# Norm sums with tokens on partitions: root and reciprocal on a few columns, spread back by products with the identity

## The reference

```python
def rmsnorm(x, g):
    x32 = x.astype(jnp.float32)
    y = x32 * lax.rsqrt(jnp.mean(x32 * x32, axis=-1, keepdims=True) + EPS)
    return (y * g.astype(jnp.float32)).astype(x.dtype)

def layer_norm(x, g, b):
    xf = x.astype(jnp.float32)
    mu = jnp.mean(xf, -1, keepdims=True)
    var = jnp.mean(jnp.square(xf - mu), -1, keepdims=True)
    y = (xf - mu) * lax.rsqrt(var + LN_EPS) * g.astype(jnp.float32) + b.astype(jnp.float32)
    return y.astype(x.dtype)
```

## Time and profile before

| | us |
|---|---|
| median of 3 runs | 2226.37 |
| lowest and highest of them | 2225.61, 2236.63 |
| profiled execution, its own time | 2233.53 |
| profiled execution, span from first to last instruction | 2231.7 |

### The profile page before, as it was taken

The page is one execution under the profiler, slowest core; times in us unless marked ns, Lnnn a source line. Parts: engine busy times, 40 slices in busy tenths (PEclk is TensorE's granted clock), DMA queues, the critical chain, the costliest instruction groups (busy, mean ns, idle before and its releaser), DMA issues. The chain is left out here.

```text
span 2231.7 us, 36800 instructions
## 1 busy us (share of the span) xinstructions
PE 2108.8 (94%) x14195; PEld 1892.5 (85%) x14195; DVE 1483.2 (66%) x2248; ACT 1157.1 (52%) x1655; POOL 26.1 (1%) x34
## 2 busy tenths in 40 slices
PE   7999999999999999889999988999999989999997
PEld 6999897999999978779998977787778758778876
DVE  5665675665666644476564456789888466888896
ACT  4343533534444335464433336678776455777774
POOL 1000000000000020000000000000000000000000
PEclk9999999999999999999999979999999999999999
DMA  8555222654445523334454521599996514799991
GB/s 278 191 196 177 95 82 90 216 179 169 170 170 175 197 80 128 138 114 170 169 186 143 148 73 58 180 328 334 342 317 212 217 38 170 244 318 325 318 358 56
DMA packets 312310, 421.09 MB, mean 189 GB/s; under 512 B 7844, under 2 KB 266304, under 8 KB 312096
## 3 DMA queue, kind: packets, MB, share of 16 engines
q1 hardware_dynamic: 308864, 415.93, 54.5%
q10 hardware_dynamic: 2816, 2.38, 0.5%
q0 software_dynamic: 544, 1.62, 0.2%
HBM read 416.70 MB, written 1.05 MB: 187 GB/s over the span
## 5 line engine op out<-in xcount | busy, mean ns | idle before, releaser
L2816 DVE TENSOR_TENSOR w_lo<-weight_ring,w_hi 128x1024 fp32r<-128x1024 f32 x384 | 449.3, 1220 | 35.9 <-ACT w_hi L2665 31.2
L569 PE MATMUL banks<-x_hi,w_hi 128*128 128x256 f32 x1408 | 401.0, 285 | 8.5 <-DVE w_lo L522 7.7
L570 PE MATMUL banks<-x_lo,w_hi 128*128 128x256 f32 x1408 | 399.3, 284 | 0.0
L571 PE MATMUL banks<-x_hi,w_lo 128*128 128x256 f32 x1408 | 399.3, 284 | 0.0
L2665 ACT ACTIVATE w_hi<-weight_ring 128x1024 fp32r<-128x1024 f32 x384 | 382.3, 1053 | 21.4 <-PE banks L2552 21.3
L515 ACT ACTIVATE w_hi<-weight_ring 128x1024 fp32r<-128x1024 f32 x88 | 93.0, 1057 | 418.5 <-PE banks L571 418.3
L887 DVE TENSOR_TENSOR pieces<-weight_ring,pieces 128x512 fp32r<-128x512 f32 (+2 forms) x245 | 166.3, 689 | 193.8 <-ACT pieces L876 192.3
L876 ACT ACTIVATE pieces<-weight_ring 128x512 fp32r<-128x512 f32 (+2 forms) x245 | 150.9, 627 | 251.3 <-PE banks L823 244.5
L569 PEld LDWEIGHTS banks<-x_hi,w_hi 128*128 128x128 f32 x1408 | 271.2, 193 | 10.8 <-DVE w_lo L522 8.6
L570 PEld LDWEIGHTS banks<-x_lo,w_hi 128*128 128x128 f32 x1408 | 271.3, 193 | 0.1
L571 PEld LDWEIGHTS banks<-x_hi,w_lo 128*128 128x128 f32 x1408 | 271.2, 193 | 0.0
(11 more groups left out here) (367 smaller groups left out, 3907.3 us busy)
## 6 DMA issues: line engine op xcount, KB each, us to landing
weight_ring<-in_ffn_w_in SPq DMA_DIRECT2D x88, 1024.0 KB, 7.5
weight_ring<-in_moe_w_gate SPq DMA_DIRECT2D x64, 1024.0 KB, 6.6
weight_ring<-in_moe_w_up SPq DMA_DIRECT2D x64, 1024.0 KB, 9.2
weight_ring<-in_moe_w_down SPq DMA_DIRECT2D x64, 1024.0 KB, 11.1
weight_ring<-in_ffn_w_out SPq DMA_DIRECT2D x44, 1024.0 KB, 9.6
weight_ring<-in_hg_w_in SPq DMA_DIRECT2D x12, 1024.0 KB, 8.2
weight_ring<-in_fox_w_in SPq DMA_DIRECT2D x12, 1024.0 KB, 8.5
weight_ring<-in_nsa_w_in SPq DMA_DIRECT2D x10, 1024.0 KB, 7.8
```

Of the source, the lines that this page charges most:

```text
L569: pe.matmul(out, w_hi, m_hi, start=start, stop=False, skip_group_check=True)
L570: pe.matmul(out, w_hi, m_lo, start=False, stop=False, skip_group_check=True)
L571: return pe.matmul(out, w_lo, m_hi, start=False, stop=stop, skip_group_check=True)
L2816: dve.tensor_tensor(self.piece(s, p, self.w_lo), self.piece(s, p), self.piece(s, p, self.w_hi.bitcast(F32)), ALU.subtract).then_inc(sem[ki ...
```

## The change

The two operands of the sum are exchanged. Now the squares are the weights (a tile of 128 features by 128 tokens) and one column of ones is the moving operand, so that the sum of a token lands on that token's partition: the result of a norm is 128x2 (two halves of the tokens), and 128x16 for the eight heads of Hgrn2. Root and reciprocal work on those few columns. Then `spread` brings the reciprocals back to the form 128x256: one column, broadcast as 128x128 weights, times the identity as moving operand gives that column's 128 values as a row in all partitions. DVE reads this product from PSUM. In Mla ACT copies it to SBUF first. `first_root` is a root of one column, ahead of the squares, with the ACT_TABLE_LOAD in front of it. The numbers of the products of zeros change too: 26 become 2 and 18, 17 become 2 and 8, 24 become 6 and 7, 10 become 3.

```diff
+    def token_sums(self, pe, out, squares, first, last):
+        for t in range(TT):
+            ins = pe.matmul(out[:, t:t + 1], squares[:, t * P:(t + 1) * P], self.c[:, C_ONES:C_ONES + 1], start=first and t == 0,
+                            stop=last, skip_group_check=True)
+        return ins
+
+    def spread(self, pe, out, col):
+        return pe.matmul(out, col.to_broadcast([P, P]), self.ident, start=True, stop=True)
+
+    def first_root(self, act):
+        act.activation(self.root_of_eps[:], self.const(C_EPS, 1), ACT.Sqrt)
...
     def act_squares(self, act):
         k = self.k
+        k.first_root(act)
...
     def pe(self, pe):
         k = self.k
-        out = k.banks.claim(pe, f"norm{self.i}")[:, 0:T]
+        out = k.banks.claim(pe, f"norm{self.i}")
         for kk in range(KD):
             if kk % 2 == 0:
                 pe.wait_ge(k.norm_sq, 4 * self.i + kk // 2 + 1)
-            last = pe.matmul(out, k.ones, k.sq[:, kk], start=kk == 0, stop=kk == KD - 1)
+            last = k.token_sums(pe, out, k.sq[:, kk], kk == 0, kk == KD - 1)
         k.banks.filled(last, f"norm{self.i}")
-        k.keep_busy(pe, k.psum[:, 0, :], 26)
+        k.keep_busy(pe, k.psum[:, 0, :], 2)
+        out = k.banks.claim(pe, f"norm{self.i}_b")
+        pe.wait_ge(k.norm_rstd, self.i + 1)
+        for t in range(TT):
+            last = k.spread(pe, out[:, t * P:(t + 1) * P], k.rstd[:, t:t + 1])
+        k.banks.filled(last, f"norm{self.i}_b")
+        k.keep_busy(pe, k.psum[:, 0, :], 18)
...
     def dve(self, dve):
         k = self.k
         k.banks.wait_read(dve, f"norm{self.i}")
-        dve.reciprocal(k.rstd[:], k.std[:]).then_inc(k.norm_rstd, 1)
-        dve.wait_ge(k.norm_rstd, self.i + 1)
+        dve.reciprocal(k.rstd[:, 0:TT], k.std[:, 0:TT]).then_inc(k.norm_rstd, 1)
+        rstd = k.banks.wait(dve, f"norm{self.i}_b")[:, 0:T]
         for kk in range(KD):
             g = k.param[:, R_NORM + self.row * KD + kk:R_NORM + self.row * KD + kk + 1]
-            dve.scalar_tensor_tensor(out=k.xn[:, kk], in0=k.x[:, kk], scalar=g, in1=k.rstd[:],
+            dve.scalar_tensor_tensor(out=k.xn[:, kk], in0=k.x[:, kk], scalar=g, in1=rstd,
                                      op0=ALU.mult, op1=ALU.mult).then_inc(k.xn_ready, 1)
+        self.wait_xn(dve)
+        k.banks.release(dve, f"norm{self.i}_b")
...
-        out = b.claim(pe, "hg_n")[0:HG_H, 0:T]
+        out = b.claim(pe, "hg_n")
         for h in range(HG_H):
             pe.wait_ge(self.o_sq, h // 2 + 1)
-            last = pe.matmul(out, k.const(C_ROW + 7 - h, HG_H), k.sq[:, h], start=h == 0, stop=h == HG_H - 1)
+            last = k.token_sums(pe, out[:, TT * h:TT * h + TT], k.sq[:, h], h == 0, True)
...
-                k.keep_busy(pe, out, 10)
+                k.keep_busy(pe, out, 3)
                 pe.wait_ge(self.root_ready, 1)
-            for h in (2 * n, 2 * n + 1):
-                last = pe.matmul(out[:, (h % 2) * T:(h % 2 + 1) * T], k.c[0:HG_H, C_IDENT + h:C_IDENT + h + 1].to_broadcast([HG_H, P]),
-                                 self.root, start=True, stop=True)
+            for m in range(4 * n, 4 * n + 4):
+                last = k.spread(pe, out[:, (m % 4) * P:(m % 4 + 1) * P], self.root[:, m:m + 1])
...
-        if not self.memory:
-            k.keep_busy(pe, k.psum[:, 0, :], 17)
         if self.memory:
             self.memory.pe_turned(pe)
+        else:
+            k.keep_busy(pe, k.psum[:, 0, :], 2)
+        out = b.claim(pe, f"ln_b{i}")
+        pe.wait_ge(k.ln_rstd, i + 1)
+        for t in range(TT):
+            last = k.spread(pe, out[:, t * P:(t + 1) * P], k.rstd[:, t:t + 1])
+        b.filled(last, f"ln_b{i}")
+        if self.memory:
             self.memory.pe_products(pe)
+        else:
+            k.keep_busy(pe, k.psum[:, 0, :], 8)
...
-        k.keep_busy(pe, k.psum[:, 0, :], 24)
+        k.keep_busy(pe, k.psum[:, 0, :], 6)
+        pe.wait_ge(self.rstd_ready, 1)
+        for m in range(4):
+            last = k.spread(pe, k.psum[:, 1, m * P:(m + 1) * P], self.std[:, m:m + 1])
+        last.then_inc(self.rstd_spread, 1)
+        k.keep_busy(pe, k.psum[:, 0, :], 7)
...
+        act.wait_ge(self.rstd_spread, 1)
+        src = k.psum[:, 1, :].rearrange("p (m t) -> p m t", m=2)
+        act.activation(self.rstd, src, ACT.Copy).then_inc(self.rstd_copied, 1)
```

More of the change, by code:

```diff
@@ L419, in __init__ @@
         k.xn_tiles += KD
-        k.banks.plan(f"norm{self.i}")
+        k.banks.plan(f"norm{self.i}", f"norm{self.i}_b")
     def act_squares(self, act):
         k = self.k
+        k.first_root(act)
         for c in range(4):
@@ L433, in pe @@
                 pe.wait_ge(k.norm_sq, 4 * self.i + kk // 2 + 1)
-            last = pe.matmul(out, k.ones, k.sq[:, kk], start=kk == 0, stop=kk == KD - 1)
+            last = k.token_sums(pe, out, k.sq[:, kk], kk == 0, kk == KD - 1)
         k.banks.filled(last, f"norm{self.i}")
-        k.keep_busy(pe, k.psum[:, 0, :], 26)
+        k.keep_busy(pe, k.psum[:, 0, :], 2)
[5 more added lines that the diff above has]
+        k.keep_busy(pe, k.psum[:, 0, :], 18)
     def act_std(self, act):
         k = self.k
-        src = k.banks.wait(act, f"norm{self.i}")[:, 0:T]
-        k.banks.read(act.activation(k.std[:], src, ACT.Sqrt, bias=k.const(C_EPS, 1), scale=1.0 / D), f"norm{self.i}")
+        src = k.banks.wait(act, f"norm{self.i}")[:, 0:TT]
+        k.banks.read(act.activation(k.std[:, 0:TT], src, ACT.Sqrt, bias=k.const(C_EPS, 1), scale=1.0 / D), f"norm{self.i}")
     def dve(self, dve):
@@ L1004, in __init__ @@
             at += HG_H * width
-        self.root = k.std[0:HG_H]
+        self.root = k.std[:, 0:TT * HG_H]
         s = lambda n: k.s("hg_" + n)
@@ L1144, in act @@
             act.activation(k.sq[:, 2 * n:2 * n + 2], k.acc[:, 2 * n:2 * n + 2], ACT.Square).then_inc(self.o_sq, 1)
-        src = b.wait(act, "hg_n")[0:HG_H, 0:T]
-        b.read(act.activation(self.root, src, ACT.Sqrt, bias=k.const(C_EPS, 1, HG_H), scale=1.0 / P), "hg_n")
+        src = b.wait(act, "hg_n")[:, 0:TT * HG_H]
+        b.read(act.activation(self.root, src, ACT.Sqrt, bias=k.const(C_EPS, 1), scale=1.0 / P), "hg_n")
         self.act_out(act)
@@ L1703, in __init__ @@
             memory.plan_turned()
+        k.banks.plan(f"ln_b{self.i}")
+        if memory:
             memory.plan_products()
@@ L1720, in pe @@
         b.filled(last, f"ln_m{i}")
[L1721 removed]
+        out = b.claim(pe, f"ln_v{i}")
         for kk in range(KD):
@@ L1740, in act @@
             act.activation(k.sq[:, 2 * c:2 * c + 2], k.xn[:, 2 * c:2 * c + 2], ACT.Square).then_inc(k.ln_sq, 1)
-        src = b.wait(act, f"ln_v{i}")[:, 0:T]
-        b.read(act.activation(k.std[:], src, ACT.Sqrt, bias=k.const(C_LNEPS, 1), scale=1.0 / D), f"ln_v{i}")
+        src = b.wait(act, f"ln_v{i}")[:, 0:TT]
+        b.read(act.activation(k.std[:, 0:TT], src, ACT.Sqrt, bias=k.const(C_LNEPS, 1), scale=1.0 / D), f"ln_v{i}")
         if self.memory:
@@ L1769, in dve @@
         b.wait_read(dve, f"ln_v{i}")
-        dve.reciprocal(k.rstd[:], k.std[:]).then_inc(k.ln_rstd, 1)
-        dve.wait_ge(k.ln_rstd, i + 1)
+        dve.reciprocal(k.rstd[:, 0:TT], k.std[:, 0:TT]).then_inc(k.ln_rstd, 1)
+        rstd = b.wait(dve, f"ln_b{i}")[:, 0:T].unsqueeze(1).to_broadcast([P, 2, T])
         for c in range(4):
             cs = slice(2 * c, 2 * c + 2)
-            dve.tensor_tensor(k.xn[:, cs], k.xn[:, cs], k.rstd[:].unsqueeze(1).to_broadcast([P, 2, T]), ALU.mult).then_inc(k.ln_scaled, 1)
+            dve.tensor_tensor(k.xn[:, cs], k.xn[:, cs], rstd, ALU.mult).then_inc(k.ln_scaled, 1)
         dve.wait_ge(k.ln_scaled, 4 * i + 4)
+        b.release(dve, f"ln_b{i}")
         for kk in (KD - 2, KD - 1):
@@ L2350, in dve @@
         dve.wait_ge(self.std_ready, 2)
+        dve.reciprocal(self.std, self.std).then_inc(self.rstd_ready, 1)
         cq, ckv = b.at("mla_cq"), b.at("mla_ckv")
-        for out, src, row, std in ((self.cq[:, 0], cq[:, 0:T], R_MQ, 0), (self.cq[:, 1], cq[:, T:2 * T], R_MQ + 1, 0),
-                                   (self.ckv, ckv[:, 0:T], R_MKV, 1)):
-            if row != R_MQ + 1:
-                dve.reciprocal(self.std[:, std], self.std[:, std]).then_inc(self.rstd_ready, 1)
-                dve.wait_ge(self.rstd_ready, std + 1)
-            dve.scalar_tensor_tensor(out=out, in0=src, scalar=k.param[:, row:row + 1], in1=self.std[:, std],
+        dve.wait_ge(self.rstd_copied, 1)
+        for out, src, row, part in ((self.cq[:, 0], cq[:, 0:T], R_MQ, 0), (self.cq[:, 1], cq[:, T:2 * T], R_MQ + 1, 0),
+                                    (self.ckv, ckv[:, 0:T], R_MKV, 1)):
+            dve.scalar_tensor_tensor(out=out, in0=src, scalar=k.param[:, row:row + 1], in1=self.rstd[:, part],
                                      op0=ALU.mult, op1=ALU.mult).then_inc(self.latent_ready, 1)
```

16 lines of the change are left out of this document (9 added, 7 removed).

## The result

The changed kernel takes 2238.9 us (median of 20 runs) against 2231.9 for the kernel before (20 runs): ratio 1.0035, 95% interval 1.0025 to 1.0045, so 7.0 us by the medians and 5.6 to 10.0 by the interval. The forecast was 2228 and a difference of +1.9 us against a median of 2226.4; the median of before itself was 5.5 us higher with more runs. What was mis-sized is the difference.

The account below looks back on a forecast made before the run. PE, busy 94% of a 2231.7 us span, was taken as the bound; norms are chains without slack. Chain saving 9.1 against clock cost 11.0 nets +1.9: 2226.4 + 1.9 = 2228 us, own range 2222 to 2235, with rivals 2217 to 2239.

Parts of the forecast that it names:

- The chain, 9.1 us: Sums' end to scaling in six norms, Hgrn2's end and Mla: shorter roots and reciprocals save 5.9 + 0.3 + 1.6 + 1.3 us.
- The norms' term: Both RMS norms and layer norms 1, 3, 4 save 1.17 us each (5.9); layer norm 2 saves 0.3.
- Costed at nothing: Sums' pace, first root's hidden table load, DVE reading the factor from PSUM (0.3 us at most): taken as nothing.
- The clock, 11.0 us: One-column sums make PE's clock fall at six norms and Hgrn2's end: 9.0 + 2.2 + 2.6 - 2.8 us lost.
- the sums' tail and the spread: In six norms, half clock over the sums' remainder and the spread costs 1.5 us each, 9.0 in all.
- my late end: In each norm, a clock fall only at the sums' end slows the spread alone: 0.5 us.
- given back: RMS norm ahead of Hgrn2, last layer norm, Hgrn2's end: existing half-clock stretches partly pass under products of zeros, returning 2.8 us.
- routing: Behind layer norms 1 and 3, routing products of 3.9 us keep the clock down: 1.3 us each, 2.6 lost.
- memory products: Behind layer norm 2, PE's 14 us of memory products run partly at half clock: 2.2 us lost.
- The first ("the clock holds", 2217): Rival: PE's clock stays up through the sums, so the chain's 9.1 us comes off: 2217 us; chance 0.15.
- The second's total: Rival: clock falls early and stays down through sums, routing and memory products, +12.4 us on the forecast: 2241; chance 0.13.
- The third: Rival: split copies or weight pieces are late next, only half the chain's 9.1 us comes through: 2233; chance 0.10.

Follow-up runs that it names:

- wide sums: Changed kernel with the sums' moving operand widened from one column of ones to 128 in all eight places, root reading one column per tile: 2221.4 us, ratio 0.9959.
- the two with wide sums in one half only: Changed kernel with 128-column sums only in both RMS norms and the Hgrn2 end: 2235.3 us; only in the four layer norms and Mla: 2226.8 us.
- the first experiment: The run with wide sums in all eight places, against the changed kernel: 2221.4 us, ratio 0.9959 to the kernel before.

## Why the prediction was right on the mechanism and wrong on a size

From the start of a place's first squares (at the Hgrn2 end: its last) to its first scaled tile, in us, read from the timelines of the profiled executions:

| place | before | after | wide sums | gain of the chain | cost of the clock |
|---|---|---|---|---|---|
| norm ahead of Hgrn2 | 6.87 | 8.89 | 6.02 | 0.85 | 2.87 |
| norm ahead of Fox | 6.80 | 9.06 | 5.95 | 0.85 | 3.11 |
| layer norm 1 | 6.80 | 8.83 | 5.95 | 0.85 | 2.88 |
| layer norm 2 | 6.80 | 8.42 | 6.81 | 0.0 | 1.61 |
| layer norm 3 | 6.80 | 7.95 | 5.95 | 0.85 | 2.00 |
| layer norm 4 | 6.80 | 6.65 | 5.95 | 0.85 | 0.70 |
| Hgrn2 end | 7.08 | 7.47 | 5.46 | 1.62 | 2.01 |

"Gain" is before less wide sums, "cost" is after less wide sums.

Each column is one execution, and the last two (2239.7 and 2217.0 us) lie 22.8 apart, 5 more than the medians. The costs are those of this pair. In the profiled executions of the changed kernel, of the one without the first root and of the two with wide sums in one half only, the five places other than layer norm 2 appear fifteen times with one-column sums; there the cost runs from 0.5 to 3.1 us and is 2.0 on average. Layer norm 4 alone has 0.70 here and 2.45 without the first root. Layer norm 2 is a case of its own: its 1.61 is PE turning the memory rows at half clock (3.39 us against 1.91), and when the kernel with wide sums ran again the same place took 8.05, with the clock at 1.00, because PE waited 1.02 us for a weight transfer there.

- **The chain, 9.1 us: about right, in part by luck.** Six norms give 4.3 (forecast 6.2), the Hgrn2 end 1.62 and 0.24 in the heads' products (1.6), Mla 1.60 (1.3): 7.7 by the traces; by the times, 9.1 and 9.6. The norms' term was 1.9 too high, the other two 0.6 too low together, and 1.4 to 1.9 of what the times show is in no chain (by the interval, 5.6 to 12.5, it may be noise). Some of that may be the clock: its mean over the runs is 0.982 and 0.983 with wide sums, against 0.979 and 0.980 for the kernel before beside them. A norm's place is 0.85, not 1.17: from the sums' end to the scaling is 1.36 (1397.55 to 1398.91), since the root on two columns is 0.26, not 0.19, and the scaling starts 0.72 after the spread, not 0.61; and the wide sums end 0.12 later. With one-column sums the slow clock makes 1.86 of it, where I wrote 1.7. At the Hgrn2 end my own rows gave 0.35 more than the 1.6 (the spreading 4.05 against 3.7), which I did not count.
- **Costed at nothing: right.** The first root (ratio 1.0034 without it) and DVE reading PSUM (L473 x8 in 3.22 us, against 3.26 for L450 x8 from SBUF).
- **The clock, 11.0 us: the mechanism held, the size is where the prediction failed.** It measured 17.5 (2238.9 less 2221.4). Two steps of it were mis-sized. The first is "the sums' tail and the spread ... I take 1.5, nearer to the late end since the fall in the earlier trace rows came 3.6 us into such work". In three of six places of the table the fall came early, 0.6 to 0.9 us into the sums (in the slice of 1406, sums from 1405.37), and cost 2.9 to 3.1, not far below the 3.5 I gave for a fall at once. In layer norm 4, where sums began at 2222.17 and the slice of 2225 is the first below 1, it cost 0.7, my late end. The six sum to 13.2, against 9.0. One row of one execution was taken as the typical delay; the delay varies from place to place and, at one place, from execution to execution (6.40 and 4.18 us of sums ahead of Fox), and the middle of my own two bounds, 2.0, is what the fifteen average. The second step is "given back ... I take 2.8 back in all", with Hgrn2's end among the places that give back: that place cost 2.9 instead (see "Given back").
- **The balance.** By the table and the bullets below: tails 13.2 (forecast 9.0), routing 1.3 (2.6), memory products nothing (2.2), Hgrn2's end 2.9 (no term), given back nothing that I could count (2.8). That is 17.4 against 11.0: 4.2 more from the tails, 5.7 more from the giving back, 3.5 less from the products behind. That 17.4 meets the 17.5 so closely is luck, since the two executions lie 22.8 apart.
- **The products behind the norms.** Routing: 1.3 by the trace (6.96 against 5.91 in the first, 6.19 against 5.91 in the third, from the scaling to the routing's sum), forecast 2.6, and not by the way I gave. The routing products themselves take 3.8 us, against 3.9 with wide sums. What is late is their start, 3.11 and 2.3 us behind the scaling against 1.96: the eight products of zeros ahead of them take 3.51 and 2.74 us where the clock is down, and 1.89 with wide sums (timeline of its first layer norm):

```profile
1398.71 1.89 PE L317 MATMUL banks<-zeros 128*128 128x512 bf16 x8
...
1400.87 0.59 PE L2542 MATMUL banks<-w_route,x_res 128*128 128x20 f32 x4 [0.27 <-ACT x_res L1795]
```

  There PE still waits for ACT; in the changed kernel it is the zeros that ACT's tile waits for. Memory products: nothing, forecast 2.2, and my sign for it, "L1866 and L1871 taking more than 13.7 us", was not seen.
- **Given back, 2.8: not in the balance, seen in one place.** At the Hgrn2 end, which I counted among the places that give back, the fall costs 2.01 us on the chain and 0.89 on the spread, in this execution; in the profiled execution of the kernel with zeros between the norms' sums, which has none at this place, the clock stays at 1.00 there and it costs nothing. In the norm ahead of Hgrn2 the projections do run at 1.00 now, while the earlier trace rows had 0.50 there. With wide sums they do so in the table's execution, but not when that kernel ran again; the slice is

```profile
234.00:235.00 1.00, 1.00 (x7) 1.00 (x7) 0.38 (x1) 0.00 (x0) 0.00 (x0) 0.50 0.00 0
```

  Of the six profiled executions with wide sums at this norm four have such a stretch of 3.4 us at the start of the projections, some 1.7 us lost; of the four with one-column sums one has it. That fits what I wrote, that an early fall passes under zeros and something comes back; how much in all was not measured.
- **Rivals.** The first ("the clock holds", 2217) is what the wide sums then made true: 9 to 10 us below before, where it had 9.1. The second's total, slower by more than half a per cent, was not reached; its sums' tails of 2.5 are as far above the average of 2.0 as my 1.5 is below. The third fell with the first experiment.

So 9 to 10 us gained and 17 to 18 lost stand where I had 9.1 against 11.0. (Both are read off the one kernel with wide sums, so they give the 7 to 8 us measured by construction.)

## What to carry to other kernels

A product whose operands are swapped so that it streams few columns costs PE the same time and can take away its clock; where a chain is to be shortened that way, stream as many columns as the pace allows (here 128) and read one of them. Price such a change by the early fall as well as by the late one, in every place, and not by the delay that one row shows; one execution does not give the typical delay either. Filler that fits a wait at full clock can outlast it at half clock and then delays real work. Then test the one factor before the change is thrown away: here the idea was worth 9 to 10 us and its form cost 17.

## What the runs showed of the hardware

- Float32 instructions with 128x128 weights take 0.118 us each with one column (3.79 us for 32, nearly all at clock 1.00) and 0.119 with 128 (3.81 for 32, at 1.00). With one column the granted clock fell to 0.50 in or behind the sums of all six norms of the changed kernel; with 128 it stayed at 1.00 in all windows of the first layer norm shown, at the same busy share of PE and PEld.
- The one-column sums ahead of Fox took 6.40 us in one execution (changed kernel) and 4.18 in another (without the first root): how far into such work the clock falls is not fixed.
- Products of zeros with 512 columns, one to four one-column instructions, did not hold it: slice 223 at 0.53. At the Hgrn2 end of that same execution, 32 one-column instructions without zeros took 3.63 us and the clock stayed at 1.00, so a fall is not certain either.
- ACT reads two columns that lie 128 apart in PSUM in 0.26 us, the same as two neighbours.
